# Issuing the side loads of a two-block transformer kernel from SyncE instead of ScalarE, with an earlier slot release

## What is computed

```python
def adaln_modulation(cond, w_ada, b_ada):
    return jnp.split(jax.nn.silu(cond) @ w_ada + b_ada, N_MOD, axis=-1)

def swiglu(x, w_gu, w_down):
    gate, up = jnp.split(x @ w_gu, 2, axis=-1)
    return (jax.nn.silu(gate) * up) @ w_down

def ffn_sublayer(x, shift, scale, gate, w_gu, w_down, g, b):
    y = swiglu(modulate(x, shift, scale), w_gu, w_down)
    return deepnorm_residual(x, MACARON_WEIGHT * gate * y, g, b)
```

## Time and profile before

| | |
|---|---|
| median of 3 runs | 2601.28 us (2596.71 to 2601.5) |
| profiled execution, its own time | 2601.5 us |
| its span in the profile | 2599.7 us |
| mean granted TensorE clock | 0.985 of full speed |
| PE busy | 2500.6 us (96%) |
| DVE busy | 1729.0 us (67%) |
| ACT busy | 1219.4 us (47%) |
| DMA moved | 359.05 MB, mean 138 GB/s |

### The profile page before, as it was taken

The page is one execution under the profiler, slowest core; times in us unless marked ns, Lnnn a source line. Parts: engine busy times, 40 slices in busy tenths (PEclk is TensorE's granted clock), DMA queues, the critical chain, the costliest instruction groups (busy, mean ns, idle before and its releaser), DMA issues.

```text
span 2599.7 us, 42985 instructions
## 1 busy us (share of the span) xinstructions
PE 2500.6 (96%) x16456; PEld 2175.5 (84%) x16456; DVE 1729.0 (67%) x3440; ACT 1219.4 (47%) x2307; POOL 659.7 (25%) x598
## 2 busy tenths in 40 slices
PE   8999999998889999999999998999999999999998
PEld 6788887876777888888888887889998889998998
DVE  5896587998777786455864446666664576746766
ACT  4333326651254433325333325755555577555684
POOL 0111122012114111112111113031135543655435
PEclk9999999998989999999999999999999999999999
DMA  6664552220002564343553432237644444544444
GB/s 265 205 207 146 169 172 65 82 74 2 3 9 81 190 201 144 134 142 105 190 178 111 166 126 90 89 125 238 192 153 146 138 154 143 166 146 143 153 137 146
DMA packets 119324, 359.05 MB, mean 138 GB/s; under 512 B 13136, under 2 KB 15312, under 8 KB 118736
## 3 DMA queue, kind: packets, MB, share of 16 engines
q1 hardware_dynamic: 78800, 282.89, 32.4%
q10 hardware_dynamic: 40320, 73.42, 8.9%
HBM read 355.20 MB, written 1.05 MB: 137 GB/s over the span
## 4 chain that ended last, share of the span: by engine, by line
PE 78%; DVE 10%; ACT 5%; issue 3%; POOL 2%; DMA 1%; SPq 0%; ACTq 0%; DVEq 0%; POOLq 0%
PE ps L1958 22%; PE ps L1961 22%; PE ps L1959 21%; DVE spl L2562 1%; PE ps L2022 1%; DVE big L2780 1%; ACT spl L2316 1%; DVE big L2586 1%; DVE work L2586 1%; PE ps L2215 1%; PE ps L1983 1%; PE ps L1985 1%; PE ps L1984 1%; PE ps L2252 1%; POOL spl L3038 1%
## 5 line engine op out<-in xcount | busy, mean ns | idle before, releaser
L1958 PE MATMUL ps<-bigr,spl 128*128 128x256 f32 (+1 forms) x3846 | 1307.1, 340 | 16.8 <-DVE spl L2562 8.6
L1961 PE MATMUL ps<-bigr,spl 128*128 128x256 f32 (+1 forms) x3846 | 1288.7, 335 | 3.5 <-POOL bigr L3043 3.2
L1959 PE MATMUL ps<-bigr,spl 128*128 128x256 f32 (+1 forms) x3846 | 1286.3, 334 | 0.0
L2562 DVE TENSOR_TENSOR spl<-ring,spl 128x512 fp32r<-128x512 f32 x838 | 659.6, 794 | 556.0 <-ACT spl L2316 551.9
L2316 ACT ACTIVATE spl<-ring 128x512 fp32r<-128x512 f32 x1024 | 630.6, 627 | 662.8 <-PE ps L1961 553.3
L1958 PEld LDWEIGHTS ps<-bigr,spl 128*128 128x128 f32 x3846 | 731.4, 190 | 110.2 <-issue 13.1
L1961 PEld LDWEIGHTS ps<-bigr,spl 128*128 128x128 f32 x3846 | 731.3, 190 | 83.6 <-POOL bigr L3043 10.3
L1959 PEld LDWEIGHTS ps<-bigr,spl 128*128 128x128 f32 x3846 | 731.9, 190 | 73.5 <-issue 1.7
L3043 POOL TENSOR_TENSOR bigr<-work,bigr 128x512 fp32r<-128x512 f32 (+1 forms) x196 | 204.2, 1045 | 943.1 <-ACT bigr L2320 942.8
L3038 POOL TENSOR_TENSOR spl<-ring,spl 128x512 fp32r<-128x512 f32 x186 | 251.7, 1354 | 277.4 <-ACT spl L2316 277.0
L2320 ACT ACTIVATE bigr<-work 128x512 fp32r<-128x512 f32 (+1 forms) x224 | 117.0, 525 | 286.9 <-DVE work L2646 190.8
(11 more groups left out here) (312 smaller groups left out, 2374.9 us busy)
## 6 DMA issues: line engine op xcount, KB each, us to landing
ring<-w_stream SPq DMA_DIRECT2D x512, 512.0 KB, 3.3
big<-w_stream ACTq DMA_DIRECT2D x280, 256.0 KB, 3.2
big<-w_stream SPq DMA_DIRECT2D x16, 512.0 KB, 10.5
X<-x_t SPq DMA_DIRECT2D x2, 1024.0 KB, 15.6
cst<-consts SPq DMA_DIRECT2D x1, 1537.5 KB, 9.7
X<-mem_t SPq DMA_DIRECT2D x1, 1024.0 KB, 5.9
out_t<-X SPq DMA_DIRECT2D x8, 128.0 KB, 2.1
prm<-params SPq DMA_DIRECT2D x1, 252.5 KB, 2.9
```

The lines of the kernel that those rows point to most:

```text
L1958: pe.matmul(out, hi, x[0], start=k == 0, stop=False)
L1959: pe.matmul(out, lo, x[0], start=False, stop=False)
L1961: finish(pe.matmul(out, hi, x[1], start=False, stop=k == nk - 1), tile, key if k == nk - 1 else None)
L2562: dve.tensor_tensor(lo_half(h), raw_half(h), hi_half(h), SUB).then_inc(*sig("lo", h, by="lo_dve"))
```

## The change

`ada_load` and `cond_load` move from ACT's program to SP's, which runs the same sequence, and a slot is given back right after the vec that reads it is issued in the order, rather than one vec later. So each side load of a stretch after the first four stands one place earlier, directly behind the vec on whose end it waits.

```diff
-                coming, past, read = [], [], []
+                coming, past = [], []
...
                         yield "ada_vec", p, l, g, j, conds, slot, a, crow, past[-2:-1]
                         past.append(("ada_k", l, g, j))
-                        read.append(si)
-                        if len(read) > 1:
-                            slots.give(read.pop(0), past[-2])
+                        slots.give(si, ("ada_k", l, g, j))
                         yield CUT
-                for si, key in zip(read, past[-1:]):
-                    slots.give(si, key)
...
+            def ada_load(j, slot, free, si):
+                a = j % 2 * HC
+                w.all(free, done)
+                sp.dma_start(slot, W[n_main + j // 2][:, a:a + HC]).then_inc(*sig("ada_in", j, by=f"ada_in{si}", n=16))
+
+            def cond_load(p, r, row, free):
+                w.all(free, done)
+                sp.dma_start(row, W[n_main + r // 2][:, r % 2 * HC:r % 2 * HC + HC]).then_inc(*sig("cond_in", p, r, by="cond_in", n=16))
...
-            run({f.__name__: f for f in (start, load, load_memory, store)})
+            run({f.__name__: f for f in (start, load, ada_load, cond_load, load_memory, store)})
...
-            def ada_load(j, slot, free, si):
-                a = j % 2 * HC
-                w.all(free, done)
-                act.dma_start(slot, W[n_main + j // 2][:, a:a + HC]).then_inc(*sig("ada_in", j, by=f"ada_in{si}", n=16))
```

More of the change, by code:

```diff
@@ L2301, in cond_silu @@
                     act.activation(row[h], row[h], ACTF.Silu).then_inc(*sig("cond_row", p, s, h))
-            def ada_load(j, slot, free, si):
-                a = j % 2 * HC
-                w.all(free, done)
-                act.dma_start(slot, W[n_main + j // 2][:, a:a + HC]).then_inc(*sig("ada_in", j, by=f"ada_in{si}", n=16))
-            def cond_load(p, r, row, free):
-                w.all(free, done)
-                act.dma_start(row, W[n_main + r // 2][:, r % 2 * HC:r % 2 * HC + HC]).then_inc(*sig("cond_in", p, r, by="cond_in", n=16))
             def split_hi(h):
@@ L2522, in scalar_program @@
             run({f.__name__: f for f in (
-                tables, start, ada_load, cond_load, cond_silu, split_hi, dual, evacuate, ada_row, square, root, deviation, sqrt_table, first_scale, glu, ln_mod, ln_shift, ln_update,
+                tables, start, cond_silu, split_hi, dual, evacuate, ada_row, square, root, deviation, sqrt_table, first_scale, glu, ln_mod, ln_shift, ln_update,
                 gates_in, gates_exp, gates_ratio, short_conv, conv_silu, conv_glu, z_silu, tail_columns, turn_kv, decay, unit_turn, q_decay,
```

## The result

| | before | changed |
|---|---|---|
| median | 2601.01 us (4 runs) | 2616.02 us (2615.55 to 2622.34, 4 runs) |
| ratio | | 1.0066, 95% interval 1.0054 to 1.0079 |
| span of the profiled execution | 2599.7 us | 2612.5 us |

The changed kernel is slower by 15 us between these medians, and by 17 us by the ratio (its interval is 14 to 21 us). The forecast was 2635 us with a range of 2607 to 2662: the direction and the mechanism came true, at about half of the size (15 to 17 of 34 us).

A forecast was written before the change was run, and what follows sets the result against it. PE was taken as the bound, except DVE in the first early stretch. Losses of 19.6 + 12.1 + 1.5 + 0 (late stretches) + 0.5 = 33.7 us on 2601.5 gave 2635 us, range 2607 to 2662.

The forecast's parts named there:

- The bound, stretch by stretch: Before the change, DVE bounds the first early stretch (0.05 us of slack); PE bounds the second, DVE catching up 0.48 us a round.
- The removal counted at 0: ACT's 60.6 us of waits for vecs go, gaining 0 (at most 4 us), since DVE's 1.22 us gap stays.
- The chain, 5.33 us: Vec's end to DVE's subtraction: issue 0.52, ring load landing 4.1, rounding 0.71; less DVE's own 3.83, idle 1.50 us a round.
- The bounds of 3.1 and 4.7: Range in us for a ring load's landing time, giving DVE 0.50 to 2.10 us idle a round.
- First early stretch, 19.6 us forecast: 14 rounds: ten idle 1.50 us, two 2.11, two 0.17, all on the path; bounds 7 to 28.
- Second early stretch, 12.1 forecast: 13 rounds, each 1.02 us over PE's 10.85, less 1.17 us of slack at the start; bounds 0 to 20.
- Third early stretch: DVE is busy 102 of 144 us, so waits are mostly made up: 1.5 us lost, bounds 0 and 5.
- Last early stretch: 256 tokens, 16 vecs: 0.5 us lost, bounds -2 and 3; opening loads start earlier but stand ahead of ring loads.
- Hidden: Rival: ring and split buffers cover the late loads, about 2601 us; said to need landing below 3.3 us. Chance 0.12.
- Faster: Rival: ACT's 61 us of waits made DVE late; first stretch returns to PE's pace, about 2598 us. Chance 0.05.
- Far slower: Rival: ring loads behind side loads in one queue land in 6.4 to 6.9 us; about 2680 us. Chance 0.12.
- The rule of the Trainium skill: Cited against the forecast: by it the move costs only initiation, for which SP has room, giving 2601 us.

The follow-up runs named there:

- opening_sp: The kernel before the change, with only the cond loads and the first four side loads of each stretch on SP: 2593.71 us, ratio 0.9974.
- release_only: The kernel before the change, with only the slot given back at once and ACT still issuing the side loads: 2599.45 us, ratio 1.000.
- second profile: The changed kernel, unaltered, measured and profiled once more: 2619.25 us, ratio 1.0078 to the kernel before; profiled span 2623.7 us.
- opening_act: The changed kernel with the cond loads and the first four side loads of each stretch back on ACT: 2625.15 us, ratio 1.0096.
- move_only: The changed kernel with the old release: SP issues the side loads, a slot is given back one vec later. 2595.83 us, ratio 0.998.
- wait_only: The kernel before with the early release; SP also waits where the changed kernel's SP does, but issues no side loads: 2627.52 us, ratio 1.0104.
- behind_ring: The changed kernel, but SP holds side loads that wait for a vec until it has issued the next ring load: 2593.66 us, ratio 0.9974.
- behind_half: The changed kernel with waiting side loads held until after the next ring load, and ring chunks loaded as two halves: 2594.50 us, ratio 0.9982.

## Why the prediction was right in kind and too large

**The bound, stretch by stretch: right.** First and second early stretches pay, third and late ones don't.

**The removal counted at 0: right for what it named.** The 1.22 us gap behind the glu stayed, and opening_sp gets its gain with ACT's waits in place. In release_only ACT waits longer for vecs than before (78.2 against 49.9 us over 40 to 1010) and nothing is lost.

**The chain, 5.33 us.** The steps are in the rows above: the ring load issued 0.45 us behind the vec's end (0.52 forecast), landing 3.85 in the median (4.1), then about 0.70 to the subtraction (0.71). Sum 5.0, less 3.83 is 1.17 us a round, where I had 1.50. So the terms of the chain were sized nearly right. The median says a little too much: a few long landings (5.1) bring the mean to 4.0, and in the second profile it is 4.3. The bounds of 3.1 and 4.7 held for median and mean, not for every single load. DVE's waits in the two stretches come to 33.0 us where the sum had 39.1. That is 6 us of the 17 by which the forecast was too high (in the second profile 2.5 of 11.5). The rest lies in the terms below.

**First early stretch, 19.6 us forecast.** DVE's waits sum to 16.7 us (20.4 in the second profile), and 14.6 (19.1) of it reached PE after 2.2 (1.4) had been gained. The difference, and the 2.2 us before, is the step that is missing in the prediction: **the opening loads**. I named them only for the last stretch ("0.5, bounds -2 and 3"). SP, running ahead in the common order, issues them some 8 us before ACT did, the ring load that DVE waits for next lands in 3.3 us instead of 6.9, and DVE enters the stretch with 3.6 us of slack, where I had counted on 0.05. In a stretch bound by DVE that is time.

**Second early stretch, 12.1 forecast, 6.6 measured.** By the prediction's own sum with the measured terms: waits 16.3, less 13 x 0.48 that DVE is faster than PE, less the slack at the start, is 6.6 for a slack of 3.5. That 3.5 is what closes the sum. The trace of the changed kernel has 4.1 us at the half where I had read 1.17. So the slack was mis-sized by about 3 us. The early opening explains about 1 us of that: opening_act and release_only, where ACT issues the opening loads as before, have 3.05 and 3.2 us at the same half. The rest belongs to the one execution that I had read, in which the last side load of that opening took 9.5 us to land, against 7.2 and 8.8 in those two. That is argued from three traces and was not tested. Of the 5.5 us by which this term was too high, some 3 come from the waits (1.25 us a round where I had 1.50) and the rest from the slack.

**Third early stretch: 0**, where I had 1.5. **Last early stretch: 2.0 gained**, at the lower bound, where I had a loss of 0.5.

Together: 14.6 - 2.2 + 6.6 - 2.0 = 17.0 us in the first profile, and 22 in the second, against the 33.7 forecast. The measured 15 us between the medians also holds parts outside all side work, of either sign; I didn't settle those. The granted clock of the mixer's stretch was 0.93 there and 0.91 in the profile before and in the second one of the changed kernel, which lacked the gain.

**The rivals.** Hidden: right for five stretches of seven. Its condition was stated wrongly, though: by the prediction's own chain, landing has to stay below 2.6 us, not 3.3, to cost nothing in the first stretch, and below 3.1 in the second. Faster: its mechanism (ACT's waits) isn't there, but a gain of 6 us was to be had by another, which the change took and then lost behind its own wait. Far slower: ring loads of 7 us and more occur, right behind an opening burst, but those that the chain goes through took 5.1 us at most in the first early stretch and 5.5 in the second (5.7 and 5.5 in the second profile). The rule of the Trainium skill (DMA: Bandwidth & Descriptors, "Issuing engines are not separate DMA queues"), that issuers share the same DMA engines and that spreading loads over them saves issue time alone, is not contradicted in what it says: move_only, with everything on SP, loses nothing. That section says nothing of a wait in the issuer's queue, and wait_only shows 27 us from waits that issue nothing.

## What to carry to other kernels

Here SP's queue ran in order, waits included (wait_only, 27 us): put a load that must wait for a late consumer behind the urgent loads of the same place, not ahead of them, or let it wait for something older. Work it out as a chain (event, issue, landing, first use) against what the consumer has to do in the same time. It costs only where the engine at the end of the chain has no slack, and that has to be read stretch by stretch. When moved loads start a stretch, look also at where their burst falls: in the first early stretch the same 2 MB cost 4 us when they went out beside the ring load needed next, and nothing when they went out 8 us earlier.

The best versions here are behind_ring and opening_sp, both at 2594 us against 2600 (ratios 0.9974). Their intervals overlap with those of behind_half and move_only, so among the four none is shown to be the best.

## What was not expected

A 512 KB load issued at the same moment as a 256 KB load of another engine landed later than one issued 0.43 us behind such a load by the same engine: 4.18 against 3.85 us (medians of 14). With the other engine's load 0.65 us ahead, before the change, the same loads took 4.08. It is not simply a matter of the queue: in behind_ring a side load of SP also goes out 0.43 us ahead of these ring loads, and they take 4.39 us. What makes the difference was not tried. And the granted clock moved between 0.91 and 0.93 in the mixer's stretch (526 to 790 us) of kernels whose instructions there are the same, beside differences of up to 4 us in that part.
